# The expert layer of a two-block network: wide gate and up blocks, down blocks of four consecutive rows a partition, and new code at the layer's two ends

## The chip, the cores and the metric

The kernel runs on one core of a Trainium2 chip, as one program. The metric is the device time of one execution in microseconds (us). The kernel before took 2612.45 us in the median of 3 runs (2610.32 to 2614.62). All data are 32-bit floats.

## The reference

The program computes two blocks of two layers each on 256 tokens of width 1024. The first block (dilated attention with a gated scan, then a gated scan) and most of the second (a delta rule, sparse attention, a dense feed-forward in layer 0) are untouched by the change. What matters is the last layer's end, a mixture of 8 experts with inner width 3584, of which every token uses two:

```python
def swiglu(h, w1, w3, w2):
    return (jax.nn.silu(h @ w1) * (h @ w3)) @ w2

def moe_ffn(h, w_router, w1, w3, w2):
    logits = (h @ w_router).astype(jnp.float32)
    top_val, top_idx = lax.top_k(logits, TOP_K)
    top_w = jax.nn.softmax(top_val, -1)
    combine = jnp.sum(jax.nn.one_hot(top_idx, N_EXPERTS, dtype=jnp.float32) * top_w[..., None], -2)
    out = jnp.zeros_like(h)
    for e in range(N_EXPERTS):
        out = out + combine[..., e:e + 1].astype(h.dtype) * swiglu(h, w1[e], w3[e], w2[e])
    return out

x = x + g_m * y
h = rms_norm(x, norm_ffn[l]) * (1.0 + sc_f) + sh_f
x = x + g_f * moe_ffn(h, w_router[0], w1_moe[0], w3_moe[0], w2_moe[0])
```

## The kernel before

Each engine has its own program, written by hand, and semaphores tie them together; `need(eng, name)` waits for the next count of a semaphore. Weights stream through RING, seven slots of 2 MiB (16 KB on each of 128 partitions). SyncE issues one transfer per slot and first waits until TensorE has counted the block in that slot as used (`item_used`).

**Head of the layer.** When the mixer's output has been added to x (DVE, L2282 and L2284), `pe_entry` spreads a row of the gate, scales x by its norm and turns it into HT with features on partitions (L1312, L1320, L1344, L1368). `pe_router` (L2292) multiplies HT with the router's weights. `dve_router` chooses two experts per token, TensorE counts tokens per expert and places (L2297 to L2301), and VectorE sorts the experts by their load (L2353 to L2356). SyncE reads the first and the last rank into registers and issues the first transfers (L2847). VectorE then builds selection matrices, TensorE gathers the chosen tokens with them (L2435) and ScalarE writes them to HTG (L2442).

**Turns.** One turn computes a pair: the fullest expert left (`which` 0) and the emptiest (`which` 1). Each has 64 wide slots; their two products run side by side in TensorE, 64 columns each. The fuller one has extra slots besides, 64 in turn 0 and 32 in later turns, whose products are cut in 2 or 4 parts that run side by side. With these inputs there are four turns, 0 to 3; turn 0 is written out, the others are a loop. A turn goes over 7 groups of 512 inner features. For each: gate block (L2555 wide, L2568 extra), up block (the same lines), Silu on ScalarE (L2643), product on VectorE (L2682), turning by TensorE (L2575), a copy to HIDT by ScalarE (L2651), and, one group later, the down block (L2584 wide, L2594 extra). A turn has 42 blocks of 2 MiB, four turns 168. Between the groups lie small pieces: the scatter of the turn before (L2450, added by VectorE in L2456), the turning of the weighted selection (L2612) and the gather for the turn after (L2435).

**Tail.** After the last turn come a rendezvous of all engines, four scatter pieces, four additions, a product with the gate row (L2701), the sum with x (L2703) and one store of 1 MiB (L2870).

Of the kernel before, what the change touches and what calls it, by code (L numbers as in the profile page):

```python
# [15 lines left out]
P = 128  # L16
# [60 lines left out]
def constants():  # L77
# [19 lines left out]
    f[:, C_SLOT:C_SLOT + P] = c  # L97
# [26 lines left out]
def network(nc, I, const_f, const_m, const_hot, const_times, out, upto=9):  # L124
    ctx = ExitStack()
    with ctx:
# [124 lines left out]
        EXTRA = (P // 2, P // 4)  # L251
        turn_items = []
# [559 lines left out]
        def pe_first(pe):  # L812
# [12 lines left out]
            pe.wait_ge(sem("padded"), 1)  # L825
# [40 lines left out]
        def act_first(act):  # L866
# [29 lines left out]
            for d in range(2):  # L896
                act.wait_ge(sem("gate_abs"), d + 1)
                act.activation(z_log[d], z_log[d], ACT.Exp)
            act.drain()
            for d in range(2):  # L900
                act.activation(z_log[d], z_log[d], ACT.Ln, bias=1.0).then_inc(sem("gate_log"), 1)
# [30 lines left out]
        def dve_first(dve):  # L932
# [8 lines left out]
            for d in range(2):  # L941
# [6 lines left out]
                dve.scalar_tensor_tensor(z_log[d], gla_g[d], -1.0, gla_g[d], ALU.mult, ALU.min).then_inc(sem("gate_abs"), 1)  # L948
            for d in range(2):
                dve.wait_ge(sem("gate_log"), d + 1)  # L950
                dve.scalar_tensor_tensor(gla_g[d], gla_g[d], 0.0, z_log[d], ALU.min, ALU.subtract)
# [82 lines left out]
        def act_second(act):  # L1034
            act.wait_ge(sem("lower_diff"), 1)
            act.activation(lb, lower[:, 0, :], ACT.Exp).then_inc(sem("lower_exp"), 1)
# [42 lines left out]
        def dve_second(dve):  # L1079
            take_turned(dve, HT, KC)  # L1080
            dve.tensor_tensor(lower[:, 0, :], lower[:, 0, :], lower[:, 1, :], ALU.subtract)\
                .then_inc(sem("lower_diff"), 1)
            dve.wait_ge(sem("lower_exp"), 1)
# [93 lines left out]
        chosen1 = keep(N_EXP)  # L1177

# [5 lines left out]
        by_rank = keep(2 * NT * N_EXP).rearrange("p (k t e) -> p k t e", k=2, t=NT)  # L1184
# [68 lines left out]
        ACTED = [ROW[:, 0:512], ROW[:, 512:768]]  # L1253
        HIDT = [ROW[:, 1024:2048].rearrange("p (b q s) -> p b q s", b=2, q=4), ROW[:, 768:1024]]
# [5 lines left out]
        PERMUTED = FREE[:, 1600:1664].rearrange("p (r e) -> p r e", r=N_EXP)  # L1260
# [112 lines left out]
        def dve_positions(dve):  # L1373
# [23 lines left out]
            dve.drain().then_inc(sem("angles"), 1)  # L1397
            need(dve, "sines")

        def act_positions(act):  # L1400
            need(act, "angles")
            for k in range(2):
                act.activation(trig[k], trig[k], ACT.Sin)
            act.drain().then_inc(sem("sines"), 1)
# [5 lines left out]
        ENTRY = [[(0, 8), (1, 0)], [(1, 6), None]]  # L1410
# [642 lines left out]
        def dve_mixer(dve, l):  # L2053
# [213 lines left out]
            for hf in range(2):  # L2267
# [7 lines left out]
                e.then_inc(sem("ym_ready"), 1)  # L2275
            for t in range(NT):
# [5 lines left out]
                dve.tensor_tensor(MIXED[:, t, :], PSA[:, t, :], GATE_ROW, ALU.mult)  # L2282
                dve.drain()
                dve.tensor_tensor(X[:, t, :], X[:, t, :], MIXED[:, t, :], ALU.add).then_inc(sem("x_ready"), 1)  # L2284
# [3 lines left out]

        def pe_router(pe):
            for t in range(NT):  # L2290
                for c in range(KC):
                    mm = pe.matmul(PSB[:, 0, N_EXP * t:N_EXP * t + N_EXP], HT[:, c, P * t:P * t + P], router_w[:, c, :],  # L2292
                                   start=(c == 0), stop=(c == KC - 1))
            mm.then_inc(sem("logits"), 1)
            need(pe, "chosen")

            pe.matmul(PSB[:, 1, 0:8], CF[:, C_BEFORE:C_BEFORE + P], chosen[:, 0, :], start=True, stop=True)  # L2297
            pe.matmul(PSB[:, 1, 8:16], CF[:, C_BEFORE:C_BEFORE + P], chosen[:, 1, :], start=True, stop=False)
            pe.matmul(PSB[:, 1, 8:16], CF[:, C_ONE:C_ONE + P], chosen[:, 0, :], start=False, stop=True)
            for t in range(NT):  # L2300
                mm = pe.matmul(PSB[:, 1, 16:24], CF[:, C_ONE:C_ONE + P], chosen[:, t, :], start=(t == 0), stop=(t == NT - 1))  # L2301
            mm.then_inc(sem("places"), 1)
            need(pe, "places_taken")

        def act_router(act):
            need(act, "top_diff")
            act.activation(top_w[:, :, 1], top_w[:, :, 1], ACT.Exp)
            act.drain().then_inc(sem("top_exp"), 1)

        def dve_router(dve):  # L2310
            need(dve, "logits")
            dve.tensor_copy(logits, PSB[:, 0, 0:16].rearrange("p (t e) -> p t e", t=NT))
            dve.drain()
            for t in range(NT):
                dve.max(top8[:, t, :], logits[:, t, :])
            dve.drain()
            for t in range(NT):
                dve.max_index(top_i[:, t, :].bitcast(U32), top8[:, t, :], logits[:, t, :])

            dve.tensor_tensor(top_w[:, :, 1], top8[:, :, 1], top8[:, :, 0], ALU.subtract)  # L2320
            dve.drain().then_inc(sem("top_diff"), 1)
            dve.tensor_copy(top8, top_i.bitcast(U32))
            place = CF[:, C_EXP:C_EXP + N_EXP]
            dve.drain()
            for t in range(NT):
                dve.tensor_scalar(chosen1, place, top8[:, t, 0:1], None, ALU.is_equal)
                dve.drain()
                dve.scalar_tensor_tensor(chosen[:, t, :], place, top8[:, t, 1:2], chosen1, ALU.is_equal, ALU.add)
                dve.drain()
            dve.drain().then_inc(sem("chosen"), 1)  # L2330
            need(dve, "top_exp")
# [5 lines left out]
            for k in range(2):  # L2337
                dve.memset(t_weight[k], 0.0)
                dve.memset(t_place[k], -1e9)
# [585 lines left out]
```

## Time and profile before

| | |
|---|---|
| median of 3 runs | 2612.45 us |
| profiled execution | 2612.26 us |
| its span, first to last instruction | 2610.5 us |
| TensorE busy | 2460.1 us, 94% |
| VectorE busy | 614.0 us, 24% |
| ScalarE busy | 455.7 us, 17% |
| transfers of the queue of weights | 576.93 MB |
| mean granted TensorE clock | 0.972 |

The page cuts the span in 40 slices of 65.3 us. The expert layer fills the slices from 27 on. A chain of waits goes back from the last instruction to what released it; inside the expert layer it follows whichever of TensorE and the transfers came last. Issue in such a chain is time for which the profile shows no cause. The state of the TensorE clock is told as a share of full speed.

### The profile page before, as it was taken

Reading aid. Unit: us, or ns where it says so; the run is one execution under the profiler, and the core shown is the slowest. Engines: PE = TensorE matmul, PEld = TensorE weight load, DVE = VectorE, ACT = ScalarE, POOL = GpSimd, SP = SyncE. Lnnn points to the kernel's source line nnn. Section 1 sums busy time; section 2 is a strip of 40 time slices with the busy share of each in tenths; the row PEclk is TensorE's granted clock in tenths of the full one; section 3 lists DMA queues with packets and bytes.
Section 4 is the critical chain, followed back from the end, with each engine's and each line's share of the span. In section 5 each row is a group of like instructions: output and inputs, shape, how many; then the busy total and the mean of one; then the engine's idle time right before and its main releaser. Section 6 shows DMA issues by size and latency. Waiting matters only on the chain.

```text
span 2610.5 us, 36347 instructions
## 1 busy us (share of the span) xinstructions
PE 2460.1 (94%) x15945; PEld 1437.8 (55%) x15945; DVE 614.0 (24%) x1457; ACT 455.7 (17%) x949; POOL 48.2 (2%) x67
## 2 busy tenths in 40 slices
PE   7999999999999999999999999799999889989987
PEld 5754776756685547777677655444443334333333
DVE  1241556713444320000144332300000001001001
ACT  1321123322213310000122142200010000001000
POOL 3300000000000000000000000000000000000000
PEclk9999899998999999999999999799999999999999
DMA  8633633327224137434532521399999999999995
GB/s 255 127 129 105 233 133 137 129 105 258 67 99 161 65 111 276 151 140 175 190 89 98 194 93 37 112 393 394 394 393 394 393 394 394 391 396 388 389 393 212
DMA packets 258237, 586.58 MB, mean 225 GB/s; under 512 B 14592, under 2 KB 16720, under 8 KB 258080
## 3 DMA queue, kind: packets, MB, share of 16 engines
q1 hardware_dynamic: 254304, 576.93, 60.2%
q0 software_dynamic: 3376, 5.94, 1.4%
q8 instruction: 130, 2.13, 0.3%
q10 hardware_dynamic: 400, 1.36, 0.2%
q14 instruction: 27, 0.22, 0.0%
HBM read 583.14 MB, written 1.06 MB: 224 GB/s over the span
## 4 chain that ended last, share of the span: by engine, by line
PE 84%; DMA 8%; SPq 3%; DVE 2%; ACT 1%; issue 1%; DVEq 1%; ACTq 0%
PE PSA L325 15%; PE PSB L2555 12%; PE PSA L340 10%; PE PSB L2489 7%; DMA RING<-in_w_moe 7%; PE PSA L2584 5%; PE PSA L2471 4%; PE PSB L2568 4%; PE PSA L699 3%; SPq L2847 3%; PE PSA L1278 2%; PE PSA L1901 2%; PE PSA L2594 2%; PE PSB L1470 1%; PE PSA L1852 1%
## 5 line engine op out<-in xcount | busy, mean ns | idle before, releaser
L2555 PE MATMUL PSB<-RING,Y 128*64 128x512 f32 x1792 | 399.9, 599 | 41.1 <-issue 20.8
L325 PE MATMUL PSA<-RING,HT 128*128 128x512 f32 (+1 forms) x896 | 392.5, 587 | 8.6 <-ACT Y L1441 5.0
L340 PE MATMUL PSA<-HT,RING 128*128 128x256 f32 x1216 | 277.8, 389 | 8.6 <-DMA RING<-in_w_in_ab 4.2
L2555 PEld LDWEIGHTS PSB<-RING,Y 128*64 128x64 f32 x1792 | 133.2, 138 | 270.4 <-issue 258.0
L325 PEld LDWEIGHTS PSA<-RING,HT 128*128 128x128 f32 x896 | 165.7, 191 | 183.2 <-issue 178.0
L340 PEld LDWEIGHTS PSA<-HT,RING 128*128 128x128 f32 x1216 | 235.0, 195 | 45.1 <-issue 11.7
L2584 PE MATMUL PSA<-RING,ROW 128*64 128x512 f32 x896 | 198.4, 595 | 5.6 <-issue 4.3
L2489 PE MATMUL PSB<-HT,RING 128*128 128x256 f32 x896 | 199.8, 381 | 2.0 <-DMA RING<-in_w_dense 2.0
L2489 PEld LDWEIGHTS PSB<-HT,RING 128*128 128x128 f32 x896 | 171.2, 191 | 37.2 <-issue 12.4
L2682 DVE TENSOR_TENSOR ROW<-ROW,PSB 128x512 f32<-128x512 f32 (+2 forms) x56 | 28.2, 504 | 589.7 <-PE PSB L2555 553.0
L2568 PE MATMUL PSB<-RING,Y 128*32 128x128 f32 (+1 forms) x3136 | 132.9, 289 | 0.0
L2568 PEld LDWEIGHTS PSB<-RING,Y 128*32 128x32 f32 (+1 forms) x3136 | 103.8, 114 | 52.3 <-issue 39.0
L2584 PEld LDWEIGHTS PSA<-RING,ROW 128*64 128x64 f32 x896 | 64.5, 137 | 120.2 <-issue 118.4
L2651 ACT ACTIVATE ROW<-PSB 128x512 f32<-128x512 f32 (+2 forms) x56 | 25.1, 450 | 503.0 <-PE PSB L2575 502.9
L2471 PE MATMUL PSA<-RING,PROJ 128*128 128x512 f32 x224 | 100.5, 592 | 0.0
L2508 DVE TENSOR_TENSOR PROJ<-PROJ,PSB 128x256 f32<-128x256 f32 x28 | 11.8, 421 | 277.2 <-PE PSB L2489 277.2
L2643 ACT ACTIVATE ROW<-PSB 128x512 f32<-128x512 f32 (+2 forms) x56 | 25.2, 450 | 283.9 <-PE PSB L2555 213.3
L1278 PE MATMUL PSA<-RING,small 128*32 128x512 f32 x384 | 57.1, 748 | 11.8 <-DVE X L709 5.0
L699 PE MATMUL PSA<-RING,HT 128*128 128x512 f32 x128 | 61.3, 634 | 5.1 <-ACT HT L383 5.1
L2471 PEld LDWEIGHTS PSA<-RING,PROJ 128*128 128x128 f32 x224 | 42.6, 190 | 42.1 <-issue 40.7
L2594 PE MATMUL PSA<-RING,ROW 128*32 128x512 f32 (+1 forms) x448 | 65.6, 597 | 0.0
L353 ACT ACTIVATE PROJ<-PSA 128x1024 f32<-128x1024 f32 x33 | 33.7, 1021 | 158.7 <-PE PSA L340 80.6
(444 smaller groups left out, 2256.8 us busy)
## 6 DMA issues: line engine op xcount, KB each, us to landing
RING<-in_w_moe SPq DMA_DIRECT2D x168, 2048.0 KB, 20.1
RING<-in_w_ada SPq DMA_DIRECT2D x24, 2048.0 KB, 8.1
RING<-in_w_dense SPq DMA_DIRECT2D x21, 2048.0 KB, 11.9
RING<-in_w_in SPq DMA_DIRECT2D x20, 2048.0 KB, 11.6
RING<-in_w_in_c SPq DMA_DIRECT2D x15, 2048.0 KB, 8.0
RING<-in_w_in_ab SPq DMA_DIRECT2D x10, 2048.0 KB, 15.6
RING<-in_w_out SPq DMA_DIRECT2D x4, 2048.0 KB, 7.8
RING<-in_w_out_ab SPq DMA_DIRECT2D x3, 2048.0 KB, 7.8
```

Of the source, the lines that this page charges most:

```text
L325: mm = pe.matmul(PSA[:, lane[k], 512 * t:512 * t + cols], HT[:, c, P * t:P * t + P], W[:, c, 0:cols], start=(c == 0), stop=(c == KC - 1))
L340: mm = pe.matmul(PSA[:, lane[k], S * j:S * j + S], W[:, c, P * j:P * j + P], HT[:, c, :], start=(c == 0), stop=(c == KC - 1))
L699: mm = pe.matmul(PSA[:, t, 512 * hf:512 * hf + 512], YT4[:, c, P * t:P * t + P], W[:, c, 512 * hf:512 * hf + 512], start=(first and c == 0 ...
L1278: mm = pe.matmul(PSA[r:r + 32, lane[k], 512 * a:512 * a + 512], cT[:, c:c + 1].broadcast_to([P, 32]), W[:, c, :], start=(c < 4), stop=(c > ...
L1901: mm = pe.matmul(PSA[:, t, 512 * hf:512 * hf + 512], YMT[:, 4 * n + c, P * t:P * t + P], W[:, c, 512 * hf:512 * hf + 512], start=(n == 0 a ...
L2471: mm = pe.matmul(PSA[:, t, 512 * hf:512 * hf + 512], HID[k % 2][:, P * t:P * t + P], W[:, q, 512 * hf:512 * hf + 512], start=(k == 0), sto ...
L2489: mm = pe.matmul(PSB[:, 2 * which + k % 2, 0:S], W[:, c, P * q:P * q + P], HT[:, c, :], start=(c == 0), stop=(c == KC - 1))
L2555: mm = pe.matmul((UP if up else GATE)[WIDE * which:WIDE * which + WIDE, :], HTG[:, c, WIDE * which:WIDE * which + WIDE], W[which][:, c, :] ...
L2568: mm = pe.matmul(BOTH[ec * j:ec * j + ec, c0:c0 + pw], HTG[:, c, P:P + ec], W[:, c, pw * j:pw * j + pw], start=(c == 0), stop=(c == KC - 1))
L2584: mm = pe.matmul(OUT[0][WIDE * which:WIDE * which + WIDE, 512 * hf:512 * hf + 512], HIDT[0][:, g % 2, q, WIDE * which:WIDE * which + WIDE] ...
L2594: mm = pe.matmul(OUT[1][ec * j:ec * j + ec, 512 * hf:512 * hf + 512], hid[:, b, j, :], W[0][:, q, 512 * hf:512 * hf + 512], start=(g == 0 ...
L2847: sp.dma_start(slot_view(j), src).then_inc(sem(f"slot_loaded{j % SLOTS}"), 16)
```

## The change

**Wide blocks.** `STAGES` puts groups in twos (0 and 1, 2 and 3, 4 and 5, and 6 alone). A gate or up block holds 512 input features by 1024 inner features (it was 1024 by 512); two such blocks, `kh` 0 and 1, make the two groups of a stage. Group 6 keeps its old shape. **Down blocks** hold the same 512 rows of `w2`, but row 4p + k lies on partition p (it was row 128k + p). For that the inner features are taken in steps of four when hidden values are turned, and, for the extra slots, when weights enter TensorE.

```diff
-        for g in range(GROUPS):
-            turn_items += [(1, "gate", g), (0, "gate", g), (1, "up", g), (0, "up", g)]
-            turn_items += [(1, "down", g - 1), (0, "down", g - 1)] if g else []
-        turn_items += [(1, "down", GROUPS - 1), (0, "down", GROUPS - 1)]
+        for u, stage in enumerate(STAGES):
+            for kind in ("gate", "up"):
+                turn_items += [(which, kind, (u, kh)) for kh in range(len(stage)) for which in (1, 0)]
+            if u:
+                turn_items += [(which, "down", g) for g in STAGES[u - 1] for which in (1, 0)]
+        turn_items += [(which, "down", g) for g in STAGES[-1] for which in (1, 0)]
...
                     if kind == "down":
-                        src = w[:, 512 * g:512 * g + 512, :].rearrange("a (k p) n -> p (a k) n", p=P)
+                        src = w[:, 512 * g:512 * g + 512, :].rearrange("a (p k) n -> p (a k) n", p=P)
                     else:
-                        src = w[:, :, 512 * g:512 * g + 512].rearrange("a (k p) n -> p (a k) n", p=P)
+                        u, kh = g
+                        rows_, cols = D // len(STAGES[u]), 512 * len(STAGES[u])
+                        src = w[:, rows_ * kh:rows_ * kh + rows_, 1024 * u:1024 * u + cols].rearrange("a (k p) n -> p (a k) n", p=P)
...
+            def first(kind, u, kh):
...
+                if kind == "gate" and kh == 0:
+                    if u:
+                        pe.wait_ge(sem("moe_turned_taken0"), each(turn, STAGES[u - 1][-1]))
+                        pe.wait_ge(sem("moe_turned_taken1"), staged(turn, u - 1))
+                    else:
+                        pe.wait_ge(sem("misc_free"), pieces(turn, 0 if begun else SCATTERS))
+                if kind == "up" and kh == 0:
+                    pe.wait_ge(sem("moe_silu0"), each(turn, STAGES[u][-1]))
...
+                            mm = pe.matmul(WIDE_BANKS[i][WIDE * which:WIDE * which + WIDE, :],
+                                           HTG[:, c, WIDE * which:WIDE * which + WIDE], W[which][:, c - per * kh, 512 * i:512 * i + 512],
...
+                            mm = pe.matmul(EXTRA_BANK[ec * j:ec * j + ec, i, 0:pw], HTG[:, c, P:P + ec],
+                                           W[0][:, c - per * kh, 512 * i:512 * i + 512]
+                                           .rearrange("k (f q) -> k q f", q=4)[:, pw // P * j:pw // P * (j + 1), :],
...
+            def turned_wide(u):
+                for i, g in enumerate(STAGES[u]):
+                    pe.wait_ge(sem("moe_hidden0"), each(turn, g))
+                    for q in range(4):
+                        mm = pe.transpose(WIDE_BANKS[i][:, P * q:P * q + P], ACTED[0][:, i, q:512:4], ident)
```

On TensorE, turn 0, from the first gather on (PSB and PSA are banks of PSUM, Y holds HTG, ROW and PROJ the hidden values, 64 and 32 are stationary columns), before:

```order
L2435 MATMUL PSB<-HT,X 128x192 x16
L2555 MATMUL PSB<-RING,Y 64x512 x16
L2568 MATMUL PSB<-RING,Y 64x256 x16
L2555 MATMUL PSB<-RING,Y 64x512 x16
L2568 MATMUL PSB<-RING,Y 64x256 x16
L2575 MATMUL PSB<-CF,ROW 128x128 x6
```

and of the change:

```order
L2628 MATMUL PSB<-RING,Y 64x512 x16
L2637 MATMUL PSB<-RING,Y 64x256 x16
L2628 MATMUL PSB<-RING,Y 64x512 x16
L2637 MATMUL PSB<-RING,Y 64x256 x16
L2647 MATMUL PSB<-CF,PROJ 128x128 x8
L2663 MATMUL PSA<-RING,ROW 64x512 x16
L2677 MATMUL PSA<-RING,PROJ 64x512 x8
L2663 MATMUL PSA<-RING,ROW 64x512 x16
L2677 MATMUL PSA<-RING,PROJ 64x512 x8
L2654 MATMUL PSB<-CF,PROJ 128x128 x4
```

The multiplications keep their sizes. Transposes and down blocks now come in twos, once in a stage, and the extra transposes (L2654) stand last, right ahead of the next stage's gate.

On SyncE the transfer of a down block is before

```order
L2847 DMA RING<-in_w_moe 128x4x1024
```

and of the change

```order
L2958 DMA RING<-in_w_moe 128x4096
```

The four pieces of a partition have become one.

**Head.** The last layer's second `pe_entry` and its rendezvous are gone. While the mixer ends, VectorE prepares the router's weights, scaled by the norm's gain and by 1 + sc_f, and their product with the shift. Raw x is turned, and the logits are multiplied by the reciprocal norm afterwards. Counts and ranking come first, then the places, then the weights of the choice. The gate row is made after the places.

```diff
+        def dve_moe_prepare(dve):
...
+            dve.tensor_tensor(router_w[:, :, :], router_w[:, :, :], md[:, 8:16].unsqueeze(2).broadcast_to([P, KC, N_EXP]), ALU.mult)
+            dve.tensor_copy(SPREAD, md[:, 16:24].unsqueeze(2).broadcast_to([P, KC, P])).then_inc(sem("gate_spread"), 1)
...
+                dve.scalar_tensor_tensor(logits[:, t, :], PSA[:, 0, 512 * t:512 * t + N_EXP], rms_x[:, t:t + 1], router_shift,
+                                         ALU.mult, ALU.add)
...
+            dve.scalar_tensor_tensor(rank_key, COUNTS, float(N_EXP), place, ALU.mult, ALU.subtract)
+            dve.drain()
+            dve.max(rank_sorted, rank_key)
+            dve.drain()
+            dve.max_index(rank_i.bitcast(U32), rank_sorted, rank_key)
+            dve.drain().then_inc(sem("ranked"), 1)
```

**Tail.** The loop ends one turn earlier, and the last turn is written out a third time, without gathers. Its last two blocks are loaded in halves of 512 columns, and each half is multiplied, scaled by the gate row and scattered by itself. In every turn the gate row is now applied to an expert's rows (YG) before the scatter, ACC starts as x, and the result is stored in four pieces.

```diff
-            act.activation(YG[0], OUT[0], ACT.Copy).then_inc(sem("moe_rows"), 1)
+                for k in range(2):
+                    e = dve.tensor_tensor(YG[k], OUT[k], GATE_ROW, ALU.mult)
...
+            for hf in range(2):
+                pe.wait_ge(sem(f"last_columns{hf}"), 32)
+                down_wide(GROUPS - 1, (512 * hf,), False)
+                down_extra(GROUPS - 1, (512 * hf,)).then_inc(sem("last_rows"), 1)
+            pe.wait_ge(sem("misc_free"), pieces(turn, SCATTERS + 1))
+            for piece in LAST_PIECES:
+                pe.wait_ge(sem("moe_rows"), turn + (piece % 2 + 1))
+                scatter_piece(pe, piece, piece).then_inc(sem("last_rows"), 1)
...
-            sp.dma_start(out[0].rearrange("(t p) f -> p t f", p=P), X[:, :, :]).then_inc(sem("out_stored"), 16)
+            for n, piece in enumerate(LAST_PIECES):
+                t, cols = piece // 2, slice(512 * (piece % 2), 512 * (piece % 2) + 512)
+                sp.wait_ge(sem("result"), n + 1)
+                sp.dma_start(out[0].rearrange("(t p) f -> p t f", p=P)[:, t, cols], ACC[:, t, cols]).then_inc(sem("out_stored"), 16)
```

TensorE's end (REGISTER_ALU and COMPARE_AND_BRANCH belong to waits and the loop; MODB holds YG), before:

```order
L2584 MATMUL PSA<-RING,ROW 64x512 x16
L2594 MATMUL PSA<-RING,ROW 32x512 x8
L2600 REGISTER_ALU
L2435 MATMUL PSB<-HT,X 128x160 x4
L2727 REGISTER_ALU
L2727 COMPARE_AND_BRANCH
L2450 MATMUL PSB<-MODB,HT 128x512 x8
```

and of the change:

```order
L2663 MATMUL PSA<-RING,ROW 64x512 x8
L2677 MATMUL PSA<-RING,PROJ 32x512 x4
L2663 MATMUL PSA<-RING,ROW 64x512 x8
L2677 MATMUL PSA<-RING,PROJ 32x512 x4
L2727 REGISTER_ALU
L2508 MATMUL PSB<-MODB,HT 128x512 x4
L2729 REGISTER_ALU
L2508 MATMUL PSB<-MODB,HT 128x512 x4
```

The last gather is gone, and the last down block stands in halves. Beside this, several semaphores are shared between places that used one each.

## Rows read from the trace of the kernel before

**Rows 1.** The page's 40 slices: what the transfers moved.
```profile
GB/s 255 127 129 105 233 133 137 129 105 258 67 99 161 65 111 276 151 140 175 190 89 98 194 93 37 112 393 394 394 393 394 393 394 394 391 396 388 389 393 212
```

**Rows 2.** Windows: from:to, length, busy us (instructions) by engine, PEclk, transfers' share, GB/s.
```profile
1810.80:1813.50 2.70, 2.70 (x14) 0.95 (x16) 0.00 (x0) 0.38 (x1) 0.00 (x0) 1.00 1.05 386
1854.00:1856.70 2.70, 2.70 (x16) 0.98 (x14) 0.00 (x0) 0.38 (x1) 0.00 (x0) 1.00 1.03 413
...
2000.00:2100.00 100.00, 91.64 (x780) 37.94 (x778) 3.61 (x7) 6.11 (x14) 0.00 (x0) 1.00 1.04 393
...
2560.00:2580.00 20.00, 19.92 (x160) 8.99 (x160) 0.97 (x2) 1.83 (x4) 0.00 (x0) 1.00 0.87 349
```

**Rows 3.** Timeline, head and tail: start, us, engine, line, instruction.
```profile
1674.34 0.16 DVE L2356 FIND_INDEX8 small<-small 128x8 uint32<-128x8 f32 x1
...
1676.29 43.24 SPq L2847 DMA_DIRECT2D RING<-in_w_moe  x11
...
2606.02 0.39 SPq L2870 DMA_DIRECT2D result<-X  x1
```

**Rows 4.** Chain of waits in turn 0, one group: start, us, engine, tile, line.
```profile
1714.16 7.02 PE PSB L2555 x32
1721.18 3.45 PE PSB L2568 x32
1724.63 6.87 PE PSB L2555 x32
...
1734.95 0.59 PE PSB L2575 x4
1735.54 7.02 PE PSA L2584 x32
1742.56 3.43 PE PSA L2594 x16
1745.99 0.37 PE PSB L2575 x2
```

**Rows 5.** The same chain in turn 1.
```profile
1952.35 1.91 PE PSB L2450 x4
1954.27 1.89 PE PSB L2568 x64
...
1974.51 0.26 PE PSB L2575
```

**Rows 6.** Chain of waits, the head of the layer.
```profile
1639.74 10.74 PE PSA L1901 x25
...
1651.92 1.23 DVE X L2284
...
1662.47 5.51 PE PSB L2292 x32
...
1683.51 7.69 PE PSB L2435 x32
...
1692.28 7.09 PE PSB L2555 x32
```

**Rows 7.** The page's costliest groups: ScalarE's copy; busy, mean ns, idle before.
```profile
L2651 ACT ACTIVATE ROW<-PSB 128x512 f32<-128x512 f32 (+2 forms) x56 | 25.1, 450 | 503.0 <-PE PSB L2575 502.9
```

**Rows 8.** Chain of waits, the last turn's end and the tail.
```profile
2580.40 1.63 PE PSB L2435 x12
...
2590.90 1.30 PE PSB L2435 x8
...
2593.17 7.15 PE PSB L2450 x16
2600.34 0.69 DVE PROJ L2456
...
2603.55 2.29 DVE X L2703
```

**Rows 9.** Timeline: products whose moving operand is read with a step.
```profile
1442.55 1.98 PE L1657 MATMUL PSA<-MODB,RING 64*64 64x33 f32 x31
```

More of the change, by code:

```diff
@@ L2305, in act_router @@
[L2305 to L2314, printed above, removed]
+                for cols in [slice(0, 512), slice(512, 1024)] if l and t else [slice(0, 1024)]:
+                    dve.tensor_tensor(MIXED[:, t, cols], PSA[:, t, cols], GATE_ROW[:, cols], ALU.mult)
+                    dve.drain()
+                    dve.tensor_tensor(X[:, t, cols], X[:, t, cols], MIXED[:, t, cols], ALU.add).then_inc(sem("x_ready"), 1)
@@ new lines, in dve_router, with by_rank @@
+            dve.drain()
+            halves = [slice(0, 4), slice(7, 3, -1)]
+            def by_rank(to, src):
+                for t in range(NT):
+                    dve.tensor_tensor(PERMUTED[:, t, :, :], PERMUTE, src[:, t, :].unsqueeze(1).broadcast_to([P, N_EXP, N_EXP]), ALU.mult)
+                dve.drain()
+                for which in range(2):
+                    dve.tensor_reduce(to[which][:, :, 0:4], PERMUTED[:, :, halves[which], :], AX.X, ALU.add)
+                dve.drain()
+            by_rank(t_place, e_place)
@@ L2532, in used, with pe_moe_turn @@
             return PER_TURN * turn + (STATIC + turn_at[what] + 1)
[L2534 removed]
+        def pe_moe_turn(pe, turn, end=False):
             ec = extra(turn)
@@ L2632, in pe_moe_turn @@
-            misc(SCATTERS + 2)
-            down(GROUPS - 1)
-            misc(SCATTERS + 3)
-        def act_moe_turn(act, turn):
+            for u, stage in enumerate(STAGES):
+                for kind in ("gate", "up"):
+                    for kh in range(len(stage)):
+                        first(kind, u, kh)
+                        k = MISC_AFTER.get((u, kind, kh))
+                        if k is not None and (begun or k == SCATTERS):
+                            misc(k)
+                turned_wide(u)
+                for n, g in enumerate(STAGES[u - 1] if u else ()):
+                    if u == len(STAGES) - 1 and not end:
+                        misc(SCATTERS + 1 + n)
+                    down(g)
+                turned_extra(u)
@@ new lines, in pe_moe_turn @@
+            if not end:
+                misc(SCATTERS + 3)
+                down(GROUPS - 1)
+                return
+            for hf in range(2):
+                pe.wait_ge(sem(f"last_columns{hf}"), 32)
[5 more added lines that the diff above has]
+                scatter_piece(pe, piece, piece).then_inc(sem("last_rows"), 1)
@@ L2699, in dve_moe_end @@
[L2699 to L2703 removed]
+            if not end:
+                dve.wait_ge(sem("item_used"), used(turn, (0, "down", GROUPS - 1)))
+                for k in range(2):
+                    e = dve.tensor_tensor(YG[k], OUT[k], GATE_ROW, ALU.mult)
+                e.then_inc(sem("moe_rows"), 1)
+                return
```

490 lines of the change are left out of this document (269 added, 221 removed).

## The prediction

> **What bounds the kernel now.** I read the slices first: from slice 27 of 40 on, the transfers run at 388 to 396 GB/s to the last slice but one [rows 1]. That is the expert layer: 168 blocks of 2 MiB (2.097 MB). The windows show that the rate has two levels [rows 2]: 386 GB/s while gate and up blocks (2 KB pieces) pass, 413 while down blocks (4 KB rows) do, so 5.43 and 5.08 us a block. By that the 112 and 56 blocks take 893 us. In fact the transfers run from 1676.3 [rows 3] to about 2577.8 (the window 2560:2580 moved 349/393 of 20 us' worth) [rows 2], 901.5 us, 1% more.
>
> The chain shows that TensorE is almost as full. In turn 0 a group of 512 inner features is 7.02 + 3.45 (gate, wide and extra slots) + 6.87 + 3.45 (up) + 0.59 + 7.02 + 3.43 (down) + 0.37 (transposes) = 32.2 us [rows 4], against 4 x 5.43 + 2 x 5.08 = 31.9 of transfer: balanced. In turns 1 to 3 the extra slots are half as many, 1.89 us for each of the three steps and 0.26 for their transposition [rows 5]; a group is 27.5 us, and TensorE waits: in the window 2000:2100 it is busy 91.6 of 100 us [rows 2]. So a faster stream alone is worth something only until TensorE's own pace is met. On both sides stand a head (router to first block, first block to first product) and a tail.
>
> **Head of the layer.** Before, x is final at 1653.2, the gate row is spread, x is scaled and turned, and the router's small multiplications end at 1668.0 [rows 6]; the search for the ranks ends at 1674.5 and the first block is asked for at 1676.29 [rows 3]; after 7.69 us of gathering the first product starts at 1692.28 [rows 6]. The change turns raw x, routes on weights that were scaled beforehand, and multiplies the logits by the norm afterwards; the gate row, until now spread by TensorE ahead of the turning, goes behind the ranking. New chain: tile 0 is turned from 1650.5 (8 transposes, 1.2 us by the 0.59 for 4 in rows 4), copied and routed (half of 5.51, so 2.75), until about 1655.2; tile 1 the same, 1.2 + 0.9 + 2.75, until 1660; choosing on VectorE 1.7; counts 1.2; ranks 1.0; SyncE's two register reads, 1.8 as before. The first block is asked for at about 1666.5, 10 us earlier. The preparation that moves ahead of the mixer's end lies in a wait of VectorE for TensorE's L1901. The first pair lands 2 x 5.1 + 2 us later, at 1679; the gather (about 1677.5) is now hidden behind that. The first product comes 13 us earlier. Bounds: 0, if the clock or a copy eats it, to 16.
>
> **The blocks.** Gate and up blocks become 512 rows of 1024 columns, 4 KB pieces, for 24 of 28 per turn (group 6 stays narrow): 5.08 us, since the size has its row. Down blocks become four consecutive rows a partition, 16 KB in one piece (the order says 128x4096). No row has that. Two rates give two terms: a piece costs 84.9 ns for 2 KB and 158.7 for 4 KB on each of 16 engines, so 73.8 per 2 KB and 11 fixed; for 16 KB 602 ns, 4.81 us a block. The bounds are 4.81 and 5.08 (no gain); I take 4.85, near the fit. A turn is then 24 x 5.08 + 4 x 5.43 + 14 x 4.85 = 211.5 us, before 223.2.
>
> The Trainium skill (DMA: Bandwidth & Descriptors, "Why small descriptors are slow") charges a fixed three cycles beside one per 32 bytes. By that, as an estimate, 4 KB would be only 2% quicker than 2 KB, where the windows show 7%; a turn would be 219 us and the whole some 22 us longer than my sum. I go by the windows.
>
> **TensorE's side.** The multiplications are the same in number and size: two gate steps instead of two groups. From [rows 4, 5, 8]: turn 0 is 7 x 32.2 + 0.6 + 4.6 (transposes of the weights of selection, three gathers) = 230.6; turns 1 and 2 are 7 x 27.5 + 4 x 1.91 + 5.2 = 205.6; the last has no gathers, 201.0. New is one wait: the gate of stages 1, 2 and 3 waits for both copies of the turned features, and the extra ones are turned immediately before it. Behind that wait stands all of TensorE; it lasts a copy on ScalarE (0.45 us in the mean) [rows 7] and two handovers, about 0.75 us, 3 a turn: 2.3. The wait of up for both Silus lies behind 1.89 us of extra slots, or 3.45. The gathers' last copy, about a microsecond of idle at a turn's end, is now behind the last down. Sum: 232.9 + 2 x 207.9 + 203.3 = 852 us. Bounds of the wait: 0 to 2 us each, 0 to 24.
>
> TensorE alone would end its products at 1679 + 852 = 2531. The stream: in turn 0 it is held back by the seven slots; when TensorE ends that turn (1912) it is some 6 blocks ahead, 120 are left, 120 x 5.04 x 1.01 = 610, plus 1.1 for the last two pairs' halves in 2 KB pieces, 2 to land and 4.4 to multiply: 2530. Two limits that are equal add something; before, such losses were 5 to 9 us. I take 2536, before 2590.9 [rows 8].
>
> **Tail.** Before: the last products end at 2590.90, then 1.30 of a gather nobody needs, 7.15 for the four scatters, the last addition of 0.69, the gate's product and the sum with x (2.29) on VectorE [rows 8], and the store from 2606.02 [rows 3]: 19.6 us to the span's end. After: the gate multiplies the rows while the second half is multiplied, x lies in the sum from turn 0, so behind the last product stand 7.15 of scatters (the order of pieces hides VectorE's first products), one addition of 0.69, the issue and a store of a quarter (4.5 - 0.75 x 2.7 = 2.5 us) with handovers: 10.9. Gain 8.7, bounds 6 to 10.
>
> Span 2536 + 10.9 = 2547; the profiled execution took 2612.26 with a span of 2610.5, 1.8 more, and agrees with the median 2612.45. Forecast **2549 us**.
>
> **What the sum leaves at nothing: reading in steps.** To fit four consecutive rows a partition, the extra slots' weights enter TensorE with a step of four floats (L2637 of the changed kernel), and the wide features are turned with a step of four in the stationary operand (L2647). Nothing before is like it save L1657: 31 products of 33 columns, step 16, in 1.98 us [rows 9], 64 ns each. At the pace of the wide products (32 x 512 columns, two side by side, in 7.02 us: 0.86 ns a column) 33 columns are 28 ns. The other 36 are either the loading of 64 stationary columns or the step; the row can't say. So the price lies between nothing and a factor of 2.25 on the extra slots. I take nothing: every product of L1657 also loads 64 columns, so a load must be in the 64 ns. A factor of 1.5 would eat all the gain (63 of 128 us).
>
> **Rivals.**
> - The step halves the pace of the extra slots' moving operand: 14 x 3.45 in turn 0 and 42 x 1.89 after it, 128 us more; turning in steps adds up to 28 x 0.43 = 12. TensorE has no slack to hide it, and the stream merely waits: 2549 + 128 + up to 12 - 5 (only one limit is left) = 2672 to 2684. Slower. For it: 64 ns for 33 columns. Against it: the load explains them as well. The Trainium skill (SBUF — State Buffer, "Door 1: The DMA port swizzle") has lines of 16 bytes that want at least two hits, which a step of four floats does not give, though it also names four fp32 as what a stride is free for. Chance 0.23. With four streams side by side (turns 1 to 3) each fetching its own line, the factor could be four: 2830, 0.03.
> - The stream does not speed up: larger pieces only move the limit to the memory, 901.5 us again. From 1666.5 it ends at 2568; + 2 + 4.4 + 10.9 + 1.8 = 2587. For it: nothing but that the rate's cause isn't seen. Against: both levels in one execution. 0.09.
> - A small price of the step (1.2 to 1.45) or waits at their upper bound together with down blocks at 5.08: 2575 to 2606. 0.05.
> - My forecast, 2530 to 2585: 0.60.
>
> The range reaches from 2530 into the slow case: **2530 to 2680**. A measurement of this kernel tells 0.2% (5 us) from no change; faster 0.73, within it 0.02, slower 0.25.
>
> **What the profile would show.** Slices at 405 to 420 GB/s where 393 stood, windows of down blocks above 413; in the chain, L2628 x32 at 7.0 us and L2637 x64 still at 1.9 (x32 at 3.45 in turn 0), L2647 x8 at 1.2; the first block asked for near 1666, first product near 1679, last near 2536, 11 us of tail. L2637 at 3.8 and 6.9 would mean the first rival, with TensorE busy throughout and a stream with gaps; slices still at 393 the second.

## The result: 2675.85 us, slower by 2.5%

| | before | after |
|---|---|---|
| median | 2611.39 us (4 runs, 2604.19 to 2614.62) | 2675.85 us (4 runs, 2672.26 to 2678.56) |
| ratio, 95% interval | | 1.025 [1.0229, 1.0271] |
| span of the profiled execution | 2610.5 us | 2670.2 us |
| TensorE busy | 2460.1 us, 94% | 2575.5 us, 96% |
| VectorE / ScalarE busy | 614.0 / 455.7 us | 607.9 / 441.0 us |

The forecast was 2549 us. The time is what the first rival gave (2672 to 2684). First the page of the changed kernel: what the transfers moved in its 40 slices, and the costliest groups of TensorE (instructions, busy us, mean ns, idle before).

```profile
GB/s 252 121 126 139 223 113 149 138 139 194 80 119 103 98 213 190 130 189 95 221 90 73 220 64 44 409 278 329 306 357 339 401 397 326 386 404 372 345 394 222
...
L2628 PE MATMUL PSB<-RING,Y 128*64 128x512 f32 x1792 | 398.5, 597 | 16.4 <-ACT PROJ L2755 8.3
...
L2637 PE MATMUL PSB<-RING,Y 128*32 128x128 f32 (+1 forms) x3136 | 266.7, 440 | 0.0
```

The steady 393 GB/s of [rows 1] became a line that jumps between 278 and 409: the stream now waits for TensorE. The wide products (L2628) cost what they did: 398.5 us, before 399.9. The extra products (L2637) cost 266.7 us, before (L2568) 132.9. The chain of waits says the same by turns, head, turn 0, turn 2 and tail (start, us, engine, tile, line):

```profile
1660.64 12.05 DMA RING<-in_w_moe
1672.78 8.78 PE PSB L2628 x32
1681.57 7.25 PE PSB L2637 x32
1688.81 6.87 PE PSB L2628 x32
1695.68 7.25 PE PSB L2637 x32
...
2191.59 1.85 PE PSA L2677 x16
2193.44 2.92 issue
2196.36 7.09 PE PSB L2628 x32
...
2610.43 7.09 PE PSB L2628 x32
2617.51 3.80 PE PSB L2637 x60
...
2658.96 1.00 PE PSA L2677 x8
2659.96 7.08 PE PSB L2508 x16
```

A half, below, is what the extra slots compute with one gate or up block: there are 14 in turn 0 and 42 after it. The trace has two MATMUL instructions for each product of the program, so a half is 32 of them with 256 elements of the moving operand in turn 0 and 64 with 128 elements later. Against [rows 4, 5] a half went from 3.45 to 7.25 us in turn 0 and from 1.89 to 3.80 after it: 14 x 3.80 + 42 x 1.91 = 133 us. L2637 is never a wait, and "busy 96%" looks like a kernel in good health: an engine that reads slowly counts as busy. What shows it is the duration of a product of known shape.

The head and the new wait of the changed kernel, from its timeline and its list of waits (us in total, times, longest):

```profile
1639.61 6.17 PE L1905 MATMUL PSA<-RING 128*128 128x512 f32 x14
...
1660.06 30.69 SPq L2958 DMA_DIRECT2D RING<-in_w_moe  x9
```
```profile
PE PSB L2628 <- ACT PROJ L2755: 8.3, 12, 0.8
```

From the mixer's last product to the first request it is now 1645.78 to 1660.06, 14.3 us; before it was 1650.48 to 1676.29, 25.8 us [rows 6, 3].

### The profile page after: what moved, and what is told of

It reads as the page before. It is cut to its first block, busy times and chain, and to the rows that moved or that the text cites. A ratio compares the mean times of both kernels' runs of the same rounds, so it can differ in the third digit from the quotient of the medians.

```text
span 2670.2 us, 36173 instructions
## 1 busy us (share of the span) xinstructions
PE 2575.5 (96%) x15899; PEld 1464.4 (55%) x15899; DVE 607.9 (23%) x1440; ACT 441.0 (17%) x912; POOL 48.3 (2%) x67
## 4 chain that ended last, share of the span: by engine, by line
PE 94%; DMA 2%; ACT 2%; DVE 1%; issue 1%; DVEq 0%; SPq 0%; ACTq 0%
PE PSB L2628 15%; PE PSA L328 14%; PE PSA L343 10%; PE PSB L2637 10%; PE PSA L2663 7%; PE PSB L2547 7%; PE PSA L2529 4%; PE PSA L702 3%; PE PSA L2677 2%; PE PSA L1905 2%; PE PSA L1282 2%; PE PSB L2508 1%; PE PSA L1856 1%; PE PSB L1880 1%; PE PSB L1474 1%; PE PSB L1747 1%
## 5 line engine op out<-in xcount | busy, mean ns | idle before, releaser
L2628 PE MATMUL PSB<-RING,Y 128*64 128x512 f32 x1792 | 398.5, 597 | 16.4 <-ACT PROJ L2755 8.3
L2628 PEld LDWEIGHTS PSB<-RING,Y 128*64 128x64 f32 x1792 | 134.7, 137 | 259.1 <-issue 259.1
L2637 PE MATMUL PSB<-RING,Y 128*32 128x128 f32 (+1 forms) x3136 | 266.7, 440 | 0.0
L2637 PEld LDWEIGHTS PSB<-RING,Y 128*32 128x32 f32 (+1 forms) x3136 | 138.1, 130 | 138.2 <-issue 93.8
L2785 DVE TENSOR_TENSOR PROJ<-PROJ,PSB 128x512 f32<-128x512 f32 x28 | 18.2, 684 | 612.7 <-PE PSB L2628 612.7
L2749 ACT ACTIVATE ROW<-PSB 128x512 f32<-128x512 f32 x28 | 15.4, 595 | 341.2 <-PE PSB L2647 341.2
L2677 PE MATMUL PSA<-RING,PROJ 128*32 128x512 f32 (+1 forms) x448 | 65.8, 597 | 0.0
L2739 ACT ACTIVATE PROJ<-PSB 128x512 f32<-128x512 f32 x28 | 15.4, 595 | 299.7 <-PE PSB L2628 299.7
```

What stands on the lines that cost most here:

```text
L2628: mm = pe.matmul(WIDE_BANKS[i][WIDE * which:WIDE * which + WIDE, :], HTG[:, c, WIDE * which:WIDE * which + WIDE], W[which][:, c - per * kh ...
L2637: mm = pe.matmul(EXTRA_BANK[ec * j:ec * j + ec, i, 0:pw], HTG[:, c, P:P + ec], W[0][:, c - per * kh, 512 * i:512 * i + 512] .rearrange("k ...
L2677: mm = pe.matmul(OUT[1][ec * j:ec * j + ec, col:col + 512], hid[:, b, j, :], W[:, q, col:col + 512], start=(g == 0 and b == 0), stop=(g == ...
```

## Experiments

Two theories after the result. **Step**: the moving operand with a step of 16 bytes enters at half pace, and everything else goes as forecast; without it the kernel is near 2540 to 2555 us. **Rest**: part of the loss lies in the wide blocks, the 16 KB pieces or the order of stages, and hides behind the step.

### The step alone, taken away and put in

`contig`: the changed kernel, with the extra products' weights read as they lie (the extra slots get features in the wrong order).

```diff
-    W[0][:, c - per * kh, 512 * i:512 * i + 512].rearrange("k (f q) -> k q f", q=4)[:, pw // P * j:pw // P * (j + 1), :],
+    W[0][:, c - per * kh, 512 * i + pw * j:512 * i + pw * (j + 1)],
```

> The changed kernel, but the extra slots' weights enter TensorE without a step (their features come in another order, so the extra slots' results are not the reference's). Theory S (the step of four floats in the moving operand doubles the extra slots' products, and that is all that made the change slow): L2637 falls from 3.80 to 1.89 us a step and from 7.25 to 3.45 in turn 0, together 14 x 3.80 + 42 x 1.91 = 133 us; time 2540 us (2530 to 2555). Rival W (the new order with its waits and twofold banks costs as well): 2590 or more, with gaps before L2628. Rival B (wide blocks in two halves leave the stream starved): above 2570 with TensorE waiting on transfers.

Measured: 2558.08 us (2552.74 to 2562.23), 0.9785 [0.9756, 0.9814] of before. The page:

```profile
GB/s 260 130 119 120 230 135 149 106 116 248 100 68 165 66 99 267 161 160 136 119 225 86 68 203 86 7 361 414 408 394 389 411 410 409 410 411 413 414 411 282
...
L2637 PE MATMUL PSB<-RING,Y 128*32 128x128 f32 (+1 forms) x3136 | 133.1, 289 | 0.0
```

The group is back at 133.1 us and the stream mostly at 408 to 414 GB/s. The time lies 3 us above the range expected. The one edit is worth 118 us in medians, and 120 in the profiled executions from the first request to the end (1010.1 us with the step, 889.8 without). The rest of the 133 goes to limits that return. TensorE's waits for transfers are 13.1 us in all, with the step 5.1, which is the wait for the first pair alone; and one turn's end costs 4 us more (below).

`before_step4`: the kernel before, with the same step put into its extra products.

```diff
-    HTG[:, c, P:P + ec], W[:, c, pw * j:pw * j + pw],
+    HTG[:, c, P:P + ec], W[:, c, :].rearrange("k (f q) -> k q f", q=4)[:, pw // P * j:pw // P * (j + 1), :],
```

> The kernel before, and only the extra slots' weights are read with a step of four floats (order of features differs, so the extra slots' results are not the reference's). Theory S: L2568 takes 3.8 instead of 1.89 us a step, 7.25 instead of 3.45 in turn 0; turn 0 is 53 us longer, turns 1 to 3 go from 222.5 (stream) to 232 (TensorE), so 2612 + 53 + 30 = 2695 us. Rival: the doubling hangs on the new banks or the order of the tiles and not on the step: 2612.

Measured: 2706.7 us, against 2612 for the kernel before. Its page has the doubled group again, at the old line number:

```profile
L2568 PE MATMUL PSB<-RING,Y 128*32 128x128 f32 (+1 forms) x3136 | 266.4, 440 | 0.0
```

So the price belongs to the step, not to the new blocks or stages. It costs 94 us here in its one execution (83 expected) and not 133, because TensorE had idle time to lose ahead of its wide products, 41.1 us before and 4.9 now (the kernel before, then this one):

```profile
L2555 PE MATMUL PSB<-RING,Y 128*64 128x512 f32 x1792 | 399.9, 599 | 41.1 <-issue 20.8 <-DMA RING<-in_w_moe 18.3 <-ACT Y L2442 2.0
```
```profile
L2555 PE MATMUL PSB<-RING,Y 128*64 128x512 f32 x1792 | 396.7, 595 | 4.9 <-ACT Y L2442 4.9
```

### What exactly costs: five forms of the same read

All four kernels here are the changed one with another access to the same weights; as in `contig`, features are not in the reference's order. `step2` takes every second float, `pairs4` takes two neighbours and hops 16 bytes:

```diff
-    .rearrange("k (f q) -> k q f", q=4)[:, pw // P * j:pw // P * (j + 1), :],
+    .rearrange("k (h f q) -> k h q f", h=2, q=2)[...],        # step2
+    .rearrange("k (h f s r) -> k h s f r", h=2, s=2, r=2)[...],  # pairs4
```

> The changed kernel, with the extra slots' weights read with a step of two floats instead of four (which features they are is not the reference's, so the extra slots' results are wrong). The doubling is shown; this asks what it hangs on. Theory L (a line of 16 bytes must give two elements): a step of two gives two elements a line, L2637 falls back to 1.89 us a step (3.45 in turn 0), time 2558 us. Rival P (two adjacent floats, 8 bytes, must be taken together): still 3.80 and 7.25, time 2676 us. Rival G (the price grows with the step): between, 2.4 to 3.2 us.

> The changed kernel, with the extra slots' weights read in runs of two adjacent floats and a hop to the next 16 bytes (other features than the reference's in the extra slots). Theories L and P both say 1.89 us a step, 3.45 in turn 0, and 2558 us, since each line and each pair gives two elements; a rival by which every read that is not one long run costs double says 3.80 and 2676 us.

`step3` has a step of 12 bytes and `step8`, in the stages of two groups, one of 32:

```diff
+    W[0][:, c - per * kh, 512 * i:512 * i + 384].rearrange("k (f q) -> k q f", q=3)[:, 0:pw // P, :],  # step3
+    W[0][:, c - per * kh, 0:1024].rearrange("k (f q) -> k q f", q=8)[...],  # step8
```

> The changed kernel with the extra slots' moving weights read at a step of three floats (12 bytes) in place of four, from the same rows (so the extra slots get wrong features). If the price is the number of 16-byte lines that a product touches (three in four of the elements open a new line): the half takes between 3.62 and 7.25 us in the first turn, near 5.4, and near 2.8 in the others. If a line must be shared by two elements in a row for the plain rate and is slow otherwise, the slow share is counted in pairs: 3.62 to 7.25 too, above 5.4. If only steps of 16 bytes and more cost: 3.62 and 1.9, as unstepped.

> The changed kernel with the extra slots' moving weights in the stages of two groups read at a step of eight floats (32 bytes) in place of four (wrong features for the extra slots). If one element for each 16-byte line is the worst case: the half stays at 3.80 (turns 1 to 3) and 7.25 us (the first), the kernel at 2670 to 2680. If the price grows with the distance: 7 and 14 us, over 2750.

The groups of `step2`, `step3` and `step8` on their pages:

```profile
L2637 PE MATMUL PSB<-RING,Y 128*32 128x128 f32 (+1 forms) x3136 | 139.3, 293 | 0.0
```
```profile
L2637 PE MATMUL PSB<-RING,Y 128*32 128x128 f32 (+1 forms) x3136 | 203.9, 367 | 0.0
```
```profile
L2637 PE MATMUL PSB<-RING,Y 128*32 128x128 f32 (+1 forms) x3136 | 269.8, 444 | 0.0
```

And one half in turn 0 (L2637 x32; a line of L2628 stands between), from the chains of `pairs4`, `step3` and `step8`:

```profile
1753.72 3.62 PE PSB L2637 x32
```
```profile
1687.84 6.87 PE PSB L2628 x32
1694.71 5.44 PE PSB L2637 x32
```
```profile
1690.06 7.36 PE PSB L2637 x32
```

| read | 16-byte lines touched by 32 x 256 = 8192 elements | half in turn 0 | ns per line | whole kernel, us |
|---|---|---|---|---|
| plain (contig) | 2048 | 3.45 us | | 2558.08 |
| step 2 floats | 4096 | 3.63 | 0.886 | 2563.81 |
| pairs, hop of 4 | 4096 | 3.62 | 0.884 | 2562.04 |
| step 3 | 6144 | 5.44 | 0.885 | 2613.92 |
| step 4 | 8192 | 7.25 | 0.885 | 2675.85 |
| step 8 | 8192 | 7.36 | 0.898 | 2685.25 |

One number fits all stepped rows within 1.5%: 0.885 ns (with two streams side by side) for each 16-byte line touched anew, or the plain pace of 3.45 / 8192 = 0.421 ns an element where that is more. A line costs as much as 2.1 elements, so with two useful floats in each line a read is nearly free (3.63 us against 3.45, 5%) and with one it is not. A step of 32 bytes instead of 16 adds 1.5%. That it is the line and not the step that counts is said by two rows: the pairs hop over 16 bytes and pay as `step2` does, and a step of 12 bytes, less than a line, pays for just the three lines in four elements that it opens. All this is for 32-bit floats; other types were not run. `step2`, `pairs4`, `step3` and `step8` are one execution each, and their halves agree with each other within 0.01 us. The Trainium skill (SBUF — State Buffer, "Door 1: The DMA port swizzle") says that a 16-byte line needs two hits or more for the full rate and that each crossing is paid; these rows agree. Its next sentence, that four fp32 can be strided over for free, does not agree with the row of step 4 (2.10 times the plain time) if it means a step of four; by the measurement a step of two is nearly free, and four is not.

`wide_dense`: is it only the narrow streams, side by side? The step goes into the wide slots (two streams) and into layer 0's dense down products (one stream) instead, the extra products read plainly. Hidden values of the wide slots and the dense output are wrong.

```diff
-    W[which][:, c - per * kh, 512 * i:512 * i + 512],
+    W[which][:, c - per * kh, 512 * i:512 * i + 512].rearrange("k (f q) -> k q f", q=4),
...
-    W[:, q, 512 * hf:512 * hf + 512], start=(k == 0), stop=(k == CHUNKS - 1))
+    W[:, q, 512 * hf:512 * hf + 512].rearrange("k (f q) -> k q f", q=4), start=(k == 0), stop=(k == CHUNKS - 1))
```

> The extra slots read without a step, but the wide slots' weights (512 columns, two streams side by side) and the down weights of the dense layer (L2529, 512 columns, one stream on the whole array) read with a step of four floats, so columns come in another order and results are wrong. Theory S in its plain form (each stream is halved, however many run): L2628 goes from 7.02 to 14.0 us for 32, and L2529 from 100.5 us to 200; time 2558 + 112 x 7 + 100 = 3440 us. Rival N (the streams side by side share something that one alone has to itself): L2529 stays at 100 us, L2628 doubles or less.

Measured: 3064.61 us. I had counted 112 steps of 7 us and there are 56, so the expected total is wrong for both theories; the durations decide. From its chain (a wide step, then a dense down step), and the dense one again in `contig`:

```profile
2002.39 14.40 PE PSB L2628 x32
...
1206.07 7.20 PE PSA L2529 x8
```
```profile
1201.50 3.43 PE PSA L2529 x8
```

7.02 us became 14.40 and 3.43 became 7.20, factors of 2.05 and 2.10; four streams side by side (turns 1 to 3) went from 1.89 to 3.80, 2.01. One stream, two or four: each is slowed by nearly the same factor. The sum is 56 x 7.38 + 28 x 3.77 = 519 us; measured against `contig`, 506.

### The rest of the change, part by part

`kp`: the new ends and the wide blocks, but down blocks in the old layout (row 128k + p) and so no step anywhere.

```diff
-    src = w[:, 512 * g:512 * g + 512, :].rearrange("a (p k) n -> p (a k) n", p=P)
+    src = w[:, 512 * g:512 * g + 512, :].rearrange("a (k p) n -> p (a k) n", p=P)
```

> The changed kernel with the down blocks laid out as before (row 128k + p on partition p) and no steps anywhere: wide gate and up blocks and both new ends alone, the whole computation. Theory S: as the run without the step, but 56 down blocks at 4 KB pieces (5.08 us against 4.85), of which some 40 lie behind turn 0, where the stream counts: 2550 us (2538 to 2565). Rival W: 2600. If the down blocks' layout is what slows the stream in the change: this one is faster than the run without the step.

`narrow`: `kp` with gate and up blocks of 1024 by 512 again (2 KB pieces), the order of stages kept.

```diff
-    rows_, cols = D // len(STAGES[u]), 512 * len(STAGES[u])
-    src = w[:, rows_ * kh:rows_ * kh + rows_, 1024 * u:1024 * u + cols]...
+    g0 = 1024 * u + 512 * kh
+    src = w[:, :, g0:g0 + 512]...
```

> As the run before it in this list, but gate and up blocks are again 1024 rows of 512 columns (2 KB pieces), in the same order of work: what wide blocks are worth. Theory S with a rate set by the piece: a turn's stream is 28 x 5.43 + 14 x 5.08 = 223.2 us, so turns 1 to 3 are bound by it: 2569 us (2560 to 2585), about 20 above the wide one, slices at 393 GB/s. Rival: the piece doesn't matter here, since TensorE sets the pace: equal to the wide one within 5 us.

Measured: `kp` 2566.15 us (2564.64 to 2572.9), 0.9828 [0.9796, 0.986]; `narrow` 2586.25 us (2577.64 to 2588.48), 0.9903 [0.9875, 0.9931]. Their slices, `kp` first:

```profile
GB/s 259 130 127 111 238 136 140 120 117 231 100 82 151 66 99 289 138 168 127 144 202 83 69 228 66 1 401 409 402 404 387 408 401 408 408 401 408 409 401 279
```
```profile
GB/s 259 128 122 115 238 134 139 131 106 261 67 100 164 66 110 282 138 156 163 178 119 100 155 108 66 119 386 394 401 390 393 394 397 387 389 401 388 394 392 278
```

Both lie about 1 us above the range expected. The change now splits in four terms from medians: the two new ends together with the new order of stages 2612 to 2586, 26 us; wide blocks 2586 to 2566, 20; down blocks in one piece of 16 KB 2566 to 2558, 8; the step 2558 to 2676, minus 118. In the profiled executions the time from the first request to the span's end, which leaves out all that lies ahead of it, is 934.2 us before, 922.7 in `narrow`, 898.1 in `kp`, 889.8 in `contig` and 1010.1 with the step. That bears out the wide blocks (25) and the down blocks (8); by the intervals of the medians alone the 8 us could be noise. No run separates the order of stages from the ends.

### A version that keeps the gain

Three kernels more. All move the wait for the extra copy behind the wide products:

```diff
                 if kind == "gate" and kh == 0:
                     if u:
                         pe.wait_ge(sem("moe_turned_taken0"), each(turn, STAGES[u - 1][-1]))
-                        pe.wait_ge(sem("moe_turned_taken1"), staged(turn, u - 1))
...
                 mm.then_inc(sem("item_used"), 1)
+                if kind == "gate" and kh == 0 and u:
+                    pe.wait_ge(sem("moe_turned_taken1"), staged(turn, u - 1))
```

`best` keeps the 16 KB pieces and reads weights plainly; the order is mended where hidden values are turned, by products of 32 or 64 columns with a step in the stationary operand. `kp_wait` is `kp` with the moved wait. `rows2` lays two consecutive rows on a partition (8 KB pieces), so that a step of two is enough:

```diff
-    .rearrange("a (p k) n -> p (a k) n", p=P)
+    .rearrange("a (h p r) n -> p (a h) r n", p=P, r=2)
...
-    .rearrange("k (f q) -> k q f", q=4)[:, pw // P * j:pw // P * (j + 1), :],
+    .rearrange("k (h f q) -> k h q f", h=2, q=2)[...],
...
-    ACTED[0][:, i, q:512:4]
+    ACTED[0][:, i, 256 * (q // 2) + q % 2:256 * (q // 2) + 256:2]
```

> A version that computes the reference and keeps 16 KB down blocks without a step in a moving operand: the extra slots' weights enter in one run, and the permutation is made when their features are turned, by small products of 64 or 32 columns whose stationary operand has the step (which cost nothing in the wide turning, L2647 at 1.16 for 8). The wait for the extra copy stands before the extra products instead of before the wide ones. Theory: as the run without the step, 2558 us; the small products add up to 0.7 us a group to TensorE (19 us in all), the moved wait gives back 0.4 us twelve times: 2555 to 2572. If the stationary step costs after all, more than 2580.

> The changed kernel with the down blocks laid as two consecutive rows a partition (pieces of 8 KB in place of 16), so the feature order needs a step of two floats and not of four, in the extra slots' moving operand and in what is turned back; the wide slots' wait for the extra copy stands ahead of the extra products. Theory (a step of 16 bytes is what costs, 8 bytes do not, and the down blocks' piece size pays a little through the queue): extra products at 3.62 us a half in the first turn and about 2.0 in the others, pieces of 8 KB move at 415 to 430 GB/s, 2552 to 2562 us. Rival (between 4 KB and 8 KB there is nothing to be had while TensorE is busy): the time of the kernel with the old down layout, 2566 within 3. Rival (step 2 costs in turning): over 2570.

> The kernel with the old down layout, the new ends and the wide blocks, with one edit more: the wide slots' wait for the extra copy stands ahead of the extra products. If the 12 waits of 0.69 us are wholly on the path: 2566 less 8, 2556 to 2561 us. If the transfers end each stage last, the time is only waited elsewhere (DMA waits grow from 19.7 us): 2563 to 2569.

| | median (range) | ratio to before | first request to the span's end |
|---|---|---|---|
| rows2 | 2556.89 (2554.09 to 2560.23) | 0.979 [0.9767, 0.9812] | 894.0 us |
| kp_wait | 2560.83 (2557.51 to 2563.15) | 0.9808 [0.9783, 0.9833] | 895.7 |
| best | 2565.56 (2564.09 to 2569.97) | 0.9826 [0.9805, 0.9847] | 899.9 |
| kp | 2566.15 (2564.64 to 2572.9) | 0.9828 [0.9796, 0.986] | 898.1 |

All four compute what the reference does and beat both kernels. The last column is of the profiled executions. `rows2` behaves as its theory says in the products, but its gain over `kp_wait` (4 us) lies inside both intervals, so 8 KB pieces are not shown to be worth anything over 4 KB. Nor is the moved wait settled: TensorE's waits for the copies fall from 6.8 us in `kp` to 2.2 in `kp_wait`, but only 2.4 us of the last column go. `best` should have gained on `contig` (889.8 us in the last column) by the moved wait, 7.7 us, and lost instead, for two reasons. Its small products (L2657) are busy for 20.1 us where the transposes of `contig` took 7.1. And at the turn's end where the loop jumps back it has a second gap of 4.12 us (issue), 1.27 us behind the first of 4.70. Against 8 us won stand 13 and 4 lost, 9 in sum; measured 10. The small products of one stage of turn 0, from its chain, behind four wide transposes:

```profile
1720.00 0.72 PE PSB L2649 x4
1720.72 2.06 PE PSB L2657 x32
```

What TensorE still waits for in `rows2` and in `kp_wait`:

```profile
PE PSB L2627 <- DMA RING<-in_w_moe: 14.2, 7, 5.2
```
```profile
PE PSB L2627 <- DMA RING<-in_w_moe: 18.0, 9, 5.5
```

The longest of each, 5.2 and 5.5 us, is the wait for the first pair, in the head.

## Why the prediction was wrong, by its own steps

**The step that failed is "What the sum leaves at nothing: reading in steps".** It took 0 for a term that was 133 us, in durations, and 118 in time. I had the right bounds (1 to 2.25 times) and the rival with the right place, factor and time, and gave it 0.23. (The turning in steps, which that rival put at up to 12 us, cost 2, as the last section shows.) The choice of zero rested on one argument about [rows 9]: the 64 ns of a product of L1657 also hold a load of 64 columns. A single stream pays 7.20 us / (8 x 512) = 1.76 ns a new line by `wide_dense`, 58 ns for its 33 elements. But products without any step, of 64 columns with a load of 64, take as long in the kernel before: these run two side by side, so each stream has 30 of them in 1.91 us, 64 ns each:

```profile
1439.81 1.91 PE L1470 MATMUL PSB<-RING 64*64 64x64 f32 x60
```

So the row of L1657 can't tell, as the text said, and then the value belongs in the middle or the chance near one half, not at the end that makes the sum nice. What should have weighed was the asymmetry: on an engine that bounds, a factor of two on 133 us against all other gains of 63.

**Head: right within 2 us.** Forecast 16.0 us from the mixer's end to the first request, measured 14.3; then 12.5 to the first product, measured 12.7. The absolute times moved because the mixer ends at another time in each execution (first requests of the changed kernel's relatives, `wide_dense` aside, lie between 1652.9 and 1669.4), which no profile of one execution can foresee.

**The new wait: right.** Forecast 0.75 us, 3 a turn, 9 us; measured 12 of 0.69, 8.3 us.

**TensorE's sum: right.** Forecast 852 us from the first product to the last scatters; measured 2659.96 - 1672.78 = 987.2, less 133 is 854. Two parts of it were wrong and small. After TensorE's wait of 5.1 us for the first pair, the first 32 wide products take 8.78 us at a granted clock of 0.81, where the others take 7.02 (granted clock third from the end):

```profile
1672.78:1681.57 8.79, 8.79 (x34) 3.50 (x36) 0.00 (x0) 0.00 (x0) 0.00 (x0) 0.81 1.02 408
```

And a turn's end was to have no idle time. That holds for turns 0 and 2, but where the loop jumps back, behind turn 1, the changed kernel has 2.92 us (issue). `contig` has 4.64, after which the clock drops; its chain, and its windows:

```profile
2122.48 4.64 issue
2127.12 9.55 PE PSB L2628 x32
```
```profile
2120.00:2125.00 5.00, 2.48 (x20) 0.42 (x16) 2.35 (x2) 0.00 (x0) 0.00 (x0) 1.00 1.03 410
2125.00:2130.00 5.00, 2.88 (x8) 1.03 (x10) 0.00 (x0) 0.00 (x0) 0.00 (x0) 0.53 1.02 407
```

The granted clock of 0.53 is almost wholly the lower level, 1.2 GHz; the wide products that took 7.02 us take 9.55. Together 7 us at one turn's end. What makes the gap is not shown.

**The blocks: nearly right, where they could act.** A turn of 42 blocks was put at 211.5 us and 1% more; at `contig`'s 412 GB/s it is 42 x 2.097 / 0.412 = 213.8, the same. The parts are less good. 16 KB pieces had 4.85 us a block; at a turn's end in the changed kernel six down blocks follow one another in the stream, and two windows in which it moved nothing but pieces of 16 KB give

```profile
2375.00:2385.00 10.00, 9.44 (x70) 3.88 (x66) 0.00 (x0) 0.98 (x2) 0.00 (x0) 1.00 0.99 421
2385.00:2395.00 10.00, 10.00 (x89) 3.99 (x84) 0.47 (x1) 0.28 (x1) 0.00 (x0) 1.00 1.01 426
```

4.92 to 4.98 us, between my value and "no gain" (5.08). The fit through two points (2 and 4 KB) overstates what a piece of 16 KB gains. The estimate by the Trainium skill (DMA: Bandwidth & Descriptors, "Why small descriptors are slow"), 2% from 2 to 4 KB, was too small: `narrow`, of which a third of the blocks already has pieces of 4 KB, moves 386 to 401, and `kp` mostly 401 to 409.

**The meeting of two limits: too cheap.** I put 5 us on it. `contig`, the kernel of my sum, took 889.8 us from the first request to the span's end, where the sum had 2547 - 1666.5 = 880.5. The 9 us are the turn's end with its clock, 7, and the waits for transfers behind the first product, 13.1 - 5.5 = 7.6 against my 5.

**Tail: right.** From the last product's end forecast 10.9, measured 2670.2 - 2659.96 = 10.2; before 19.6.

## What to carry to other kernels

Before weights are laid out so that transfers are long, write down how many useful bytes TensorE finds in each 16-byte line of what it reads as the moving operand: with one float it ran at half pace here, with two at nearly full. A permutation costs far less in the stationary operand of transposes that are there anyway (some 2 us in `contig`, by the numbers below), or take so few rows a partition that a step of two is enough. When a new access pattern stands on the engine that bounds and no row prices it, price it at the worse bound until a run has measured it: the share of busy time will not show it afterwards.

## What the runs showed of the hardware

- The moving operand pays per 16-byte line: a stream takes 1.76 ns a line against 0.84 ns an element (7.20 and 3.43 us for 8 x 512). With two streams side by side both change by less than 3%; with four they are 1.86 and 0.92 ns, 6% and 10% more (3.80 and 1.89 us for 64 x 128).
- A step in the stationary operand costs too, but little, since the loads lie beside products in the trace. The loads of 128 columns for the wide transposes take 211 ns in the median with a step of four (the changed kernel), 209 with a step of two (`rows2`) and 140 without (`kp`); 8 transposes take 1.16 us with the step and 1.02 without:

```profile
L2647 PEld LDWEIGHTS PSB<-CF,PROJ x112: 195/211/220, 1731.1 to 2632.4; 128*128 128x128 f32 x112
```
```profile
L2648 PEld LDWEIGHTS PSB<-CF,PROJ x112: 194/209/219, 1719.0 to 2517.2; 128*128 128x128 f32 x112
```
```profile
L2646 PEld LDWEIGHTS PSB<-CF,PROJ x112: 137/140/144, 1722.9 to 2525.0; 128*128 128x128 f32 x112
```
```profile
1791.04 1.16 PE PSB L2647 x8
```
```profile
1994.54 1.02 PE PSB L2646 x8
```

  For 112 transposes that is 2 us in all. Here two floats a line are no better than one, so the rule of the moving operand does not hold for a load.

- The transfers moved 426 GB/s over 10 us with TensorE fully busy, with pieces of 16 KB; in slices of 64 us it was mostly 401 to 409 with pieces of 4 KB, and 386 to 401 with two thirds of the blocks in pieces of 2 KB.
- An idle gap on TensorE where the loop jumps back was followed by a lower granted clock in `contig` (gap 4.64 us) and not in the changed kernel (2.92 us, 1.00 in the 5 us behind it). The length of the gap does not decide it: in `step8` it was 2.86 us, and the 5 us behind it have 0.66:

```profile
2206.80:2211.80 5.00, 5.00 (x16) 1.61 (x18) 0.00 (x0) 0.00 (x0) 0.00 (x0) 0.66 1.02 415
```
